# Weight units loaded beside row gathers, split into transfers of 120 and of 8 partitions

## The reference

```python
def peer_ffn(h, w_q, sub_keys, u, v):          # cut
    q = (xt @ w_q).reshape(T, PEER_HEADS, 2, PEER_HALF)
    sc = jnp.einsum('thcd,hckd->thck', q, sub_keys)
    ...                                        # 16 of 16384 experts per token and head
    hid = gelu(jnp.einsum('tkd,td->tk', u[ib], xb))
    return jnp.einsum('tk,tkd->td', gb * hid, v[ib])

h = h + peer_ffn(rms_norm_2(h, ffn_norm[i]), peer_w_q[i], peer_keys[i], peer_u[i], peer_v[i])
g = jax.nn.sigmoid(rms_norm_2(h, ple_norm[i]) @ ple_gate[i])     # the token gate
h = h + g * (p[i] @ ple_proj[i])
```

## Time and profile before

| | us |
|---|---|
| median of 3 runs (2343.05 to 2343.38) | 2343.07 |
| profiled execution, its own time | 2345.07 |
| its span, first to last instruction | 2343.0 |
| PE busy in the span | 2089.7 (89%) |
| DVE busy | 1745.5 (74%) |
| ACT busy | 788.4 (34%) |
| gathers' queue q0, share of 16 DMA engines | 54.8% |
| SP's queue q1, the same | 21.5% |
| row stage of layer 0, about | 760 to 1413 |
| row stage of layer 1, about | 1655 to 2307 |

### The profile page before, as it was taken

One profiled execution on the slowest core, in us unless ns is written; L12 is line 12 of the kernel. 1 busy time (PEld: TensorE's weight loads), 2 busy tenths in 40 slices (PEclk: granted clock), 3 DMA queues, 4 the chain that ended last, 5 costly groups with the idle time before them and its releaser, 6 DMA issues. The chain is left out here.

```text
span 2343.0 us, 26604 instructions
## 1 busy us (share of the span) xinstructions
PE 2089.7 (89%) x9124; PEld 1362.2 (58%) x9124; DVE 1745.5 (74%) x3737; ACT 788.4 (34%) x1479; POOL 682.8 (29%) x520
## 2 busy tenths in 40 slices
PE   8999999999999898897877788999898997787877
PEld 8998889999877544432322226988654542222224
DVE  6545765558856898978888886656888887888886
ACT  5335653336574222211211116445312121211114
POOL 0000000000100554554555540000355455455650
PEclk9999999999999999999999999999999999999999
DMA  7555425554425999999999995645899999999994
GB/s 263 190 180 179 144 90 182 192 182 148 143 106 220 390 426 427 426 427 427 427 427 427 427 392 201 215 151 217 337 423 427 427 426 427 426 427 427 427 427 182
DMA packets 101354, 726.83 MB, mean 310 GB/s; under 512 B 11632, under 2 KB 11888, under 8 KB 13424
## 3 DMA queue, kind: packets, MB, share of 16 engines
q0 software_dynamic: 74016, 539.00, 54.8%
q1 hardware_dynamic: 25200, 181.41, 21.5%
q10 hardware_dynamic: 2016, 4.89, 0.6%
HBM read 724.21 MB, written 1.05 MB: 310 GB/s over the span
## 5 line engine op out<-in xcount | busy, mean ns | idle before, releaser
L2108 PE MATMUL bank<-arena 128*128 128x512 f32 (+4 forms) x2104 | 915.0, 566 | 168.9 <-DVE arena L1987 164.8
L754 POOL DMA_INDIRECT arena<-in_uv,expert x434 | 568.7, 1310 | 836.1 <-PE bank L2108 434.1
L2108 PEld LDWEIGHTS bank<-arena 128*128 128x128 f32 (+2 forms) x2104 | 358.0, 193 | 640.7 <-DVE arena L1987 398.4
L2037 DVE SCALAR_TENSOR_TENSOR arena<-arena,xn 128x1024 f32<-128x1024 f32 x434 | 531.0, 1223 | 55.1 <-DMA arena<-in_uv,expert 52.7
L1351 DVE TENSOR_TENSOR lw_rounded<-lw,w_hi 128x2048 fp32r<-128x2048 f32 x151 | 348.3, 2308 | 197.1 <-ACT w_hi L807 193.9
L1247 ACT ACTIVATE act_h<-hid 128x1 f32<-128x1 f32 x512 | 103.7, 203 | 1009.9 <-DVE arena L2037 858.9
L2108 PE MATMUL bank<-xT_hi,w_hi 128*128 128x256 f32 x1320 | 413.0, 313 | 6.4 <-DVE xT_lo L1396 4.7
L807 ACT ACTIVATE w_hi<-lw 128x2048 fp32r<-128x2048 f32 (+1 forms) x171 | 309.2, 1816 | 233.4 <-PE bank L2108 218.1
L2108 PE MATMUL bank<-xT_lo,w_hi 128*128 128x256 f32 x1320 | 373.9, 283 | 0.0
L2108 PE MATMUL bank<-xT_hi,lw_rounded 128*128 128x256 f32 x1224 | 346.8, 283 | 0.0
L1987 DVE TENSOR_SCALAR arena<-consts,act_h,weight 128x128 f32<-128x128 f32 x512 | 200.2, 391 | 128.5 <-ACT act_h L1247 120.7
(11 more groups left out here) (270 smaller groups left out, 1992.7 us busy)
## 6 DMA issues: line engine op xcount, KB each, us to landing
lw<-in_units SPq DMA_DIRECT2D x163, 1024.0 KB, 4.8
arena<-in_uv,expert POOLq DMA_INDIRECT x434, 17.7
arena<-in_units SPq DMA_DIRECT2D x6, 1024.0 KB, 8.8
wide<-in_wide POOLq DMA_DIRECT2D x2, 1024.0 KB, 8.8
gain<-in_gains ACTq DMA_DIRECT2D x4, 512.0 KB, 10.0
wide<-in_units SPq DMA_DIRECT2D x2, 1024.0 KB, 7.0
h<-in_x SPq DMA_DIRECT2D x2, 512.0 KB, 4.4
arena<-in_ret_consts ACTq DMA_DIRECT2D x1, 1024.0 KB, 7.0
```

The source lines that it names most:

```text
L754: nc.gpsimd.indirect_dma_start(out=row_slot(slot), out_offset=None, in_=table, in_offset=bass.IndirectOffsetOnAxis(ap=expert[par][:, k:k + ...
L2037: V.scalar_tensor_tensor(row_slot(slot)[:, 0:D], row_slot(slot)[:, 0:D], 1.0, xn[:, tile, :], ALU.mult, ALU.mult, accum_out=hid[par][:, k: ...
L2108: return nc.tensor.matmul(o, lhsT, rhs, start=start, stop=stop, **more)
```

## The change

The four token gate units and the units of heads 5 and 7, in both layers, are put into a set PARTED. They are loaded by `load_parted`, which issues two transfers, one of partitions 0 to 119 and one of partitions 120 to 127, both of which add 16 to the slot's semaphore. LOADS counts such units twice, so that whoever waits for the unit waits for both. The token gate's loads are issued in the layer loop right behind the wait for the last row but two, with the same targets of `lw_used` as before; the last call of `load_units`, which did it for layer 1, becomes an assertion. Nothing else changes: the same bytes go to the same places, and no other engine has an edit other than the larger semaphore targets.

```diff
-LOADS = {u: sum(v not in WHOLE and v not in BLOCK_OF and v not in IN_SCORES for v in range(u % RING, u + 1, RING)) for u in range(UNITS)}
+
+PARTED = {first + i for first in (A_PEER0, A_PEER1) for i in (6, 8)} | {first + 1 + i for first in (A_PLE0, A_PLE1) for i in range(4)}
+PART = 120
+LOADS = {u: sum((1 + (v in PARTED)) * (v not in WHOLE and v not in BLOCK_OF and v not in IN_SCORES) for v in range(u % RING, u + 1, RING)) for u in range(UNITS)}
...
+            def load_parted(u, slot):
+                for rows in (slice(0, PART), slice(PART, P)):
+                    sp.dma_start(lw[rows, slot, :], units_d[u, rows]).then_inc(lw_loaded[slot], 16)
+
...
                     sp.wait_ge(lw_used, before + 1)
-                    load_unit(u, u % RING)
+                    (load_parted if u in PARTED else load_unit)(u, u % RING)
                 assert first == head + 10
...
                 sp.wait_ge(row_landed[SLOT_OF[layer][last]], 16 * FILLED[layer][last])
-                loaded = first
-            load_units(loaded, UNITS)
+                for u in range(first, first + 4):
+                    sp.wait_ge(lw_used, u - RING + 1)
+                    load_parted(u, u % RING)
+                loaded = first + 4
+            assert loaded == UNITS
```

## The result

The changed kernel takes 2376.2 us (median of four, 2373.3 to 2378.7) against 2343.2 for the kernel before, +33 us. The ratio of the runs is 1.0136, with a 95% interval of 1.0124 to 1.0147. I had forecast 2337.3, in a range of 2333.5 to 2350.5: the wrong side, and outside the range.

A forecast was written before the change was run, and what follows sets the result against it. Transfers were taken to bound the row stages, with one DMA engine late at their ends, and compute engines the rest. Gains of 1.9 + 2.4 + 1.5 = 5.8 us from 2343.1 gave 2337.3 us, range 2333.5 to 2350.5.

The forecast's parts named there:

- What bounds the kernel: Transfers set the pace in the two row stages, at 427 GB/s; outside them the compute engines do, at 80 to 260.
- The packets: SP's queue q1 should go from 25,200 to 25,284 packets if the 8 partitions go to eight engines.
- (1): Four more SP issues at each row stage's end make the last issue about 1.7 us later, costing nothing.
- The late engine's part is 0: The DMA engine that finishes the rows late carries 0 packets of each split unit, instead of 8.
- rival (a): The late engine isn't the one left out and keeps 8 or 9 packets per unit: 0 to +2 us; chance 0.26.
- (2): Token gate, layer 1: last row 1.23 us earlier, first unit's copy 1.9 us earlier; gain 1.9 us.
- (3): Token gate, layer 0: idle times before the last two rows go back to 0.59 us each; gain 2.4 us.
- (4): Heads 5 and 7: loads mostly fill a gap in the gathers; gain 0.5 and 1.0 us, bounds 0 and 3 together.
- Rival (b): Regrouped units' transfers lose speed, at worst 4.9 us a unit instead of 2.44: +7.5 us, 2350.6; chance 0.24.
- (5): The wait for the four gate units moves from a loop into the unrolled code, same targets: nothing.
- (c): Heads 5 and 7: no gap for the late engine, or rows won there are kept: 2329.0 us; chance 0.07.
- the heads at 3: Heads 5 and 7 gaining their upper bound of 3 us together, which gave the forecast's lower bound of 2335.7 us.

The follow-up runs named there:

- e4: The same twelve units in two transfers each, both over all 128 partitions with half of the columns, compared with the kernel before: 2344.3 against 2344.1 us, ratio 1.0000.
- e7: Only each token gate's first unit split, into sixteen transfers of eight partitions, every fourth of a group of 32, compared with the kernel before: 2356.0 against 2344.1 us.

## Why the prediction was wrong, point by point

Two steps of the sum failed: that the late engine is the one left out, so that its part is 0, and that on the other engines a unit still takes 2.44 to 2.75 us. The second one turned the gain into a loss.

**What bounds the kernel**: right. Transfers set the pace in the row stages, and what touches them there is paid in full: +14.5 and +19.1 us against 4.0 for more units elsewhere.

**The packets**: right to the packet, 25,284. **(1) the issues**: right, eight take 3.16 us, and e4 shows that they cost nothing.

**The late engine's part is 0**: wrong. After the fifteen others have finished layer 0's units in the changed kernel, from 1437 to 1440, one engine still moves packets of q1:

```profile
q1 hardware_dynamic: 10, 0.07, 5.2%
```

An engine that was left out of both transfers couldn't have any. These are eight packets of 8 KB, 0.31 us each, and two closing ones, one before the last 8 KB and one after it: the end of a part of the 120 partitions, and one packet of the 8. That this is the engine that was late with the rows shows in its last row. The row's last four packets start 1.1 to 1.2 us apart, from 1420.51 to 1424.00, though each takes 0.6, and in each of the three gaps between them a unit's packet starts and ends with the gap, within 0.03 us. e7 says the same: the late engine is one of the eight that carry the small part. So it kept its eight packets of each unit and got a ninth. This was the choice that the prediction named as open. Alone it would have cost only the gain of 5.8 us, rival (a).

**(2) and (3), the gate**: -4.3 forecast, +19.1 measured. The step "on the other engines a unit takes 2.44 us, or 2.75" failed. From 1414 to 1437 the four units needed 23 us, 5.7 each. Even on engines that had nothing else to do a packet took about 0.6 us instead of 0.31. The prediction had no row for this grouping of partitions and took the time of the old one.

**(4), the heads**: the gap is there, but a unit in it now takes twice as long and runs out of it. Before, q1 was done by 784.8; after, it shares the engines with the rows until 796, at 243 GB/s for both from 778 to 793. -1.5 forecast, +14.5 measured. I had counted 80 us of cover for the unit itself, which holds (ScalarE copies head 5's unit at 874.2), and not asked what a slow transfer does to the rows beside it.

**Rival (b)** had the mechanism, with a chance of 0.24 and a price of +7.5 us, less than a quarter of what came. What it priced, the units, was nearly right: a unit took 5.7 us where 4.9 was called the worst, and the fourth unit's copy came 4.8 and 4.2 us later behind the last row, 9.0 together. Two terms were missing. The last row was left at its old place, though it goes through the same engines and parts of the memory: in layer 0 it comes 8.81 us after the row before it, where that was 3.95, everything on ScalarE stands behind it, and the two layers lose 10.7 us by it. And the heads, 13 to 14.5 us, were priced at nothing in this rival too. Its sign came: the DMA share is still 0.93 from 2342 to 2344, so fifteen engines are busy long after 2316. Its argument against, 427 GB/s, spoke only of the grouping that the change gives up, as the prediction itself said; that should have moved weight to it, not away.

**(5) and (c)**: nothing and not seen. One bound of the sum is off by 0.1: with the heads at 3 it comes to 2335.8.

## What to carry to other kernels

A transfer's cost is not only its bytes and its count of engines: which partitions it spans decides how fast its packets go. That adjacent partitions put two engines on one part of the memory is the theory that fits all of the splits and was not seen directly. Splitting a full 128-partition transfer by partitions (120 + 8, 64 + 64, 112 + 16) cost 1.9 to 2.8 us for each 1 MB where the DMA engines were full and 0.25 where they were not, while splitting by columns cost nothing. A slower transfer in a saturated stretch is paid by everything beside it, so price it at the rate of the whole stretch, not at the slack of the data that it carries. In the DMA share of a stretch a halved rate can't be seen; the GB/s beside it show it.

## What the runs showed of the hardware

The DMA engines' busy share stayed at 0.95 to 1.02 while the rate fell from 417 to 208 GB/s. 64 packets on sixteen engines took 0.53 or 0.39 us each by the partitions that they went to. Transfers of eight partitions spaced by four took SP 0.62 us each to issue, against about 0.3 for adjacent ones. An instruction fetch held the one late engine up for 0.31 us and made the next packet 0.5 us longer. What is left open: why a lone transfer of eight adjacent partitions loses almost nothing; whether the late engine carries all of the fetches; and how the loss divides between the 120 and the 8, which was not tried, as neither can be left away alone.
